# Asking for rows of the second expert table twelve rows behind the first instead of eight

## The chip, the cores and the metric

The kernel runs on one core of a Trainium2 chip. The metric is device time in microseconds for one execution. Before the change three runs gave 4503.58, 4523.78 and 4526.52 us, a median of 4523.78 us. A further, profiled execution took 4516.98 us; all rows of the trace are from it.

## The reference, cut to what matters

The program is two blocks of a transformer-like model in float32, over 512 tokens of width 1024. What the change touches is the last part of the second block, a product-key expert layer. Each token has 8 heads that choose 16 of 16,384 experts each, so 128 experts per token. An expert is one row of 1024 numbers in table `u_tab` and one in table `v_tab`:

```
t   = h.reshape(512, 1024)
idx = e1 * 128 + e2                         # (token, head, 16) expert numbers
gate = softmax(best)                        # their weights
act = gelu(einsum('phkd,pd->phk', u_tab[idx], t)) * gate
out = einsum('phk,phkd->pd', act, v_tab[idx])
x   = x + out;  then the final rmsnorm
```

So for each token 128 rows of each table are gathered from the chip's memory: 512 x 128 x 2 rows of 4 KB, 537 MB in all. That is most of what the program moves.

## The kernel before, in words

The four tiles of 128 tokens are treated one after the other. What the code calls a row `k` (0 to 511) is one gather of 128 table rows, one for each token of a tile, 512 KB: `k // 128` is the tile, `k % 128` the expert slot. For each `k` there is a U gather, a dot product, an activation, a V gather and an accumulation. Five instruction streams run over the same count of ticks, `TICKS = range(ROWS + TILE_LAG)`, 524 of them. Each stream is in order, and waits in it hold everything behind them:

- POOL (lines 1161 to 1182): at tick `k` it asks for U row `k` (line 1167) as soon as VectorE has finished the dot of row `k-8` (semaphore `u_used`), since there are `ERING = 8` U buffers. Right behind it comes V row `v = k - V_LAG` (line 1176), as soon as TensorE has used V row `v-8` (`v_used`), since there are 8 V buffers too. At ticks 39, 71, 103 and so on, every 32 rows, `expert_numbers` (lines 1141 to 1157) computes the next 32 expert numbers on the same engine; it needs what `pair_choice` left on VectorE eight ticks before.
- VectorE, called DVE (lines 2253 to 2276): at tick `k` it waits for U row `k` to land and makes the dot products (line 2262, the product is written over the row). At each eighth tick it turns the activations of the last eight rows into weights (`acts`, line 2267). Every 32 ticks come `key_choice` and `pair_choice`, the top-16 searches.
- ScalarE, called ACT (lines 1591 to 1616): at tick `k` it builds the diagonal matrix of row `k-9` (line 1601) from `acts`; at each eighth tick it does the gelu of eight dots (line 1604).
- TensorE, called PE (lines 2801 to 2836): at tick `k = v + 11`, for even `v`, it waits until V rows `v` and `v+1` have landed and their diagonals are ready, and adds both into four banks (line 2826, the trace has 16 matmuls for a pair).
- At ticks 138 and 139, and 128 and 256 later, a tile ends: ACT's `final_swap` waits until all 128 V rows of the tile are used (line 1562), PE adds the swapped halves (line 2807), ACT's `final_root` squares them (line 1576), and DVE's `final_rows` (lines 2233 to 2246) scales and writes the rows, ahead of the dot of its tick. Only then can PE take the banks for the next tile (line 2817).

Beside the gathers, tokens 256 to 511 still have to go through the whole of the second block before their own experts are known. That work, called `side` in each stream, is spread over ticks 2 to 204 (table `SIDE`): at the end of tick `k` each of PE, DVE and ACT does its share of that tick's side steps. PE's side step of a tick often feeds DVE's of the same tick, and so on. Its weights come through SP's queue in blocks of 1 MB, into two places of the ring.

The ticks are the order in which each stream writes its work; nothing makes two streams be at the same tick but the semaphores named.

Of the kernel before, what the change touches and what calls it, by code (L numbers as in the profile page):

```python
# [170 lines left out]
ERING = 8  # L171
EXPERTS = PH * PTOPK
ROWS = NL // P * EXPERTS
V_LAG, DIAG_LAG, SUM_LAG, TILE_LAG = 8, 9, 10, 12
SCORE_LEAD, KEY_LEAD, PAIR_LEAD, NUMBER_LEAD, SHARE_LEAD = 49, 41, 33, 25, 17
SIDE_COST = {"msq": 4, "msum": 34, "mscl": 4, "lruz": 4, "ab": 20, "sp1": 10, "sp2": 10, "sp3": 15, "xr": 34, "gate": 34, "lg": 14,
             "le": 10, "ls": 15, "qkv": 34, "z": 34, "gq": 4, "gs": 6, "gr": 8, "gn": 12, "ktok": 12, "vtok": 12, "pa": 40, "pb": 40, "eye": 10,
# [2680 lines left out]
```

How the kernel before makes its waits and increments, by code:

```python
        def claim(pe, t, extra=0):  # L389
            if use_of[t] > 0:
                pe.wait_ge(S(f"bank{bank_of[t]}_free"), use_of[t] + extra)
            return ps[bank_of[t]]
# [4 lines left out]
        def filled(eng, t, extra=0):  # L398
            eng.wait_ge(S(f"bank{bank_of[t]}_full"), use_of[t] + 1 + extra)
            return ps[bank_of[t]]
# [4 lines left out]
        def emptied(eng, t, extra=0):  # L406
            eng.wait_ge(S(f"bank{bank_of[t]}_free"), use_of[t] + 1 + extra)
# [33 lines left out]
        def block(pe, b, k, extra=0, n=None):  # L442
            pe.wait_ge(S(f"weights{slot_of[b]}"), 16 * (load_of[b] + 1) + 16 * extra)
            n = n or SLOT // k
            return ring_part[slot_of[b]][:, 0:k * n].rearrange("p (k n) -> p k n", k=k)
# [7 lines left out]
            def __call__(self, eng, ins):  # L454
                self.n += 1
                ins.then_inc(S(self.name), 1)
                eng.wait_ge(S(self.name), self.n + self.off)
# [115 lines left out]
        def norm_sums(pe, tag, tbs, h, kd=KD, per=1):  # L573
            t0 = ticket0[f"norm_{tag}"]
            for b, (lo, hi) in enumerate(tbs):
                bank = claim(pe, t0 + b)
                for k in range(kd):
                    pe.wait_ge(S(f"{tag}_sq"), per * k + 1 + (b if per > 1 else 0))
                    last = pe.matmul(bank[:, 0:hi - lo], ones[:, :], h[:, k, lo:hi], start=(k == 0), stop=(k == kd - 1))
                fill(last, t0 + b)
# [558 lines left out]
            def expert_numbers(u):  # L1141
                t, j = UNITS[u]
                pool.wait_ge(S("onehot_ready"), u + 1)
                for s in range(2):
```

## Time and profile before

| | us |
|---|---|
| three runs | 4503.58, 4523.78, 4526.52; median 4523.78 |
| profiled execution, its own time | 4516.98 |
| its span | 4515.1 |
| outside the span | 1.9 |
| busy: PE, DVE, POOL, ACT | 3608.2, 1988.7, 1459.2, 965.8 |
| gather instructions on POOL: U (L1167), V (L1176) | 541.2 (512 of them), 535.0 (512 of them) |

"Busy" counts the time in which an engine executes; an engine that waits for a semaphore is idle. A gather instruction on POOL only writes the descriptors; the transfer then runs on the 16 DMA engines, and "to landing" is the time from the instruction's start to the arrival of all its bytes. The first U gather starts at 2768.5 us of the span and the last V gather at 4492.9 us.

### The profile page before, as it was taken

To read this page: it belongs to the slowest core of one execution; us is meant where nothing else is said; L and a number is where in the kernel's file an instruction comes from. 1 tells how busy PE (TensorE), PEld (TensorE's weight loads), DVE (VectorE), ACT (ScalarE), POOL (GpSimd) and SP (SyncE) were. 2 spreads that over 40 slices of the span, in tenths; PEclk is the share of its full clock that TensorE was granted. 3 is DMA by queue.
4 is the path that set the end of the run, shared out by engine and by line. 5 is a ranking of instruction groups with operands and counts; after the bars stand their busy time and mean duration, and the time that the engine had idled before them with its cause. 6 is when DMAs were issued, how large, how long until landed. Compare 5 with 4: busy or idle time off the path is not lost.

```text
span 4515.1 us, 45196 instructions
## 1 busy us (share of the span) xinstructions
PE 3608.2 (80%) x16837; PEld 2076.7 (46%) x16837; DVE 1988.7 (44%) x4450; ACT 965.8 (21%) x2181; POOL 1459.2 (32%) x1670
## 2 busy tenths in 40 slices
PE   6789998999999778999997987777787765545545
PEld 3355534555555564444466876435454521111111
DVE  2565062632232682111125214676654555555553
ACT  3564022200000211100034211342222111112111
POOL 0000001253322000000000002566666677777776
PEclk8899999999999889999998999888898987767677
DMA  4232102222113124322221223987798999899998
GB/s 175 75 112 80 56 23 49 75 107 107 71 73 139 43 104 160 113 74 74 82 88 40 94 94 129 327 314 286 279 346 333 363 346 349 340 343 354 357 361 343
DMA packets 287765, 821.56 MB, mean 182 GB/s; under 512 B 24040, under 2 KB 60341, under 8 KB 284245
## 3 DMA queue, kind: packets, MB, share of 16 engines
q0 software_dynamic: 150832, 565.17, 33.3%
q1 hardware_dynamic: 136320, 253.22, 15.7%
q8 instruction: 118, 1.93, 0.2%
q14 instruction: 75, 0.61, 0.0%
q10 hardware_dynamic: 420, 0.62, 0.0%
HBM read 791.67 MB, written 27.26 MB: 181 GB/s over the span
## 4 chain that ended last, share of the span: by engine, by line
PE 61%; DVE 13%; POOL 8%; ACT 6%; issue 6%; DMA 6%; SPq 0%; ACTq 0%; DVEq 0%; POOLq 0%
PE bank L716 24%; PE bank L2593 8%; PE bank L2826 5%; POOL arena L1176 4%; POOL ring L1167 3%; PE bank L2396 3%; PE bank L2553 2%; DVE ring L2262 2%; PE bank L2448 2%; DMA ring<-in_peer_u,arena 2%; DMA arena<-in_peer_v,arena 1%; PE bank L2688 1%; PE bank L2312 1%; PE bank L581 1%; DMA ring<-in_peer_wq 1%
## 5 line engine op out<-in xcount | busy, mean ns | idle before, releaser
L2826 PE MATMUL bank<-arena 64*64 64x512 f32 x4096 | 646.4, 762 | 452.5 <-issue 205.0
L2262 DVE SCALAR_TENSOR_TENSOR ring<-ring,xT 128x1024 f32<-128x1024 f32 x512 | 634.6, 1254 | 437.7 <-DMA ring<-in_peer_u,arena 436.3
L1176 POOL DMA_INDIRECT arena<-in_peer_v,arena x512 | 535.0, 1045 | 329.5 <-PE bank L2826 199.6
L1167 POOL DMA_INDIRECT ring<-in_peer_u,arena x512 | 541.2, 1057 | 184.8 <-issue 150.9
L2826 PEld LDWEIGHTS bank<-arena 64*64 64x64 f32 x4096 | 177.3, 162 | 842.3 <-issue 840.1
L716 PE MATMUL bank<-hT,ring 128*128 128x512 f32 (+1 forms) x1536 | 554.7, 524 | 5.1 <-ACT hT L631 5.1
L716 PE MATMUL bank<-arena,ring 128*128 128x512 f32 (+1 forms) x1536 | 551.3, 521 | 0.0
L2593 PE MATMUL bank<-hT,ring 128*128 128x256 f32 x1536 | 368.4, 400 | 62.9 <-DVE hT L2002 22.4
L716 PEld LDWEIGHTS bank<-hT,ring 128*128 128x128 f32 x1536 | 293.4, 191 | 264.6 <-issue 251.5
L716 PEld LDWEIGHTS bank<-arena,ring 128*128 128x128 f32 x1536 | 292.3, 190 | 257.7 <-issue 243.9
L1148 POOL TENSOR_TENSOR hT<-hT,arena 128x256 f32<-128x256 f32 x64 | 61.1, 985 | 1069.9 <-DVE hT L2219 1069.6
L2593 PEld LDWEIGHTS bank<-hT,ring 128*128 128x128 f32 x1536 | 303.9, 201 | 142.8 <-issue 43.1
L748 DVE SCALAR_TENSOR_TENSOR xT<-bank,modT,xT 128x512 f32<-128x512 f32 x96 | 63.5, 662 | 421.2 <-PE bank L716 421.1
L728 ACT ACTIVATE arena<-bank 128x512 f32<-128x512 f32 x96 | 50.4, 526 | 905.2 <-PE bank L716 905.1
L740 DVE TENSOR_TENSOR arena<-arena 128x512 f32<-128x512 f32 x96 | 64.6, 681 | 388.4 <-ACT arena L728 387.8
L1601 ACT ACTIVATE arena<-arena,rstd 128x64 f32<-128x64 f32 x512 | 141.0, 336 | 258.9 <-DVE rstd L2267 254.9
L1078 POOL DMA_DIRECT2D arena<-shape_consts x3 | 1.6, 535 | 414.4 <-ACT arena L1278 414.4
L2396 PE MATMUL bank<-hT,ring 128*128 128x256 f32 (+1 forms) x384 | 124.3, 486 | 0.0
L2553 PE MATMUL bank<-hT,ring 128*128 128x512 f32 x256 | 111.7, 600 | 0.0
L1604 ACT ACTIVATE rstd<-rstd 128x8 f32<-128x8 f32 x64 | 13.2, 206 | 457.0 <-DVE ring L2262 456.8
L2448 PE MATMUL bank<-arena,ring 128*128 128x512 f32 (+1 forms) x256 | 88.3, 506 | 14.6 <-DVE arena L1764 14.6
L2396 PEld LDWEIGHTS bank<-hT,ring 128*128 128x128 f32 x384 | 73.0, 190 | 51.3 <-issue 46.5
(518 smaller groups left out, 4657.9 us busy)
## 6 DMA issues: line engine op xcount, KB each, us to landing
ring<-in_mlp_w SPq DMA_DIRECT2D x32, 2048.0 KB, 8.3
ring<-in_ada_w SPq DMA_DIRECT2D x24, 2048.0 KB, 11.5
s_store<-arena POOLq DMA_DIRECT2D x8, 2816.0 KB, 9.5
ring<-in_w_in SPq DMA_DIRECT2D x10, 2048.0 KB, 8.0
arena<-s_store SPq DMA_DIRECT2D x16, 1024.0 KB, 6.5
ring<-in_w_in SPq DMA_DIRECT2D x12, 1024.0 KB, 12.9
ring<-in_w_out SPq DMA_DIRECT2D x4, 2048.0 KB, 8.1
ring<-in_s_w_glu SPq DMA_DIRECT2D x4, 2048.0 KB, 17.4
```

Source lines behind the costliest of these rows:

```text
L716: last = pe.matmul(bank[:, 0:hi - lo], w[:, k, m * P:(m + 1) * P], x[:, k, lo:hi], start=(k == 0), stop=(k == 7))
L740: dve.tensor_tensor(hid[:, m, lo:hi], hid[:, m, lo:hi], hid[:, m, lo:hi], ALU.mult)\
L748: drained(dve.scalar_tensor_tensor(xT[:, m, lo:hi], bank[:, 0:hi - lo], modT[l][:, 5 * KD + m, b:b + 1], xT[:, m, lo:hi], ALU.mult, ALU.ad ...
L1167: pool.indirect_dma_start(u_row[k % ERING], None, I["peer_u_2"][0], bass.IndirectOffsetOnAxis(idxs[:, k // EXPERTS, k % EXPERTS:k % EXPERT ...
L1176: pool.indirect_dma_start(v_row[v % ERING], None, I["peer_v_2"][0], bass.IndirectOffsetOnAxis(idxs[:, v // EXPERTS, v % EXPERTS:v % EXPERT ...
L1601: act.activation(diag[:, d % ERING, :], eye2, ACT.Copy, scale=acts[:, d % ERING:d % ERING + 1]).then_inc(S("diag_ready"), 1)
L2262: dve.scalar_tensor_tensor(row, row, 1.0, h_tok[k // EXPERTS % 2], ALU.mult, ALU.mult, accum_out=dots[k // ERING % 2][:, k % ERING:k % ERI ...
L2396: last = pe.matmul(bank[:, 0:hi - lo], w[:, k, m * P:(m + 1) * P], hT[:, k, lo:hi], start=(k == 0), stop=(k == KD - 1))
L2448: last = pe.matmul(bank[:, 0:hi - lo], w[:, k, m * P:(m + 1) * P], mixT[:, k, lo:hi], start=(k == 0), stop=(k == 7))
L2553: last = pe.matmul(bank[:, :], w[half][:, k, m * P:(m + 1) * P], hT[:, k, 0:NL], start=(k == 0), stop=(k == KD - 1))
L2593: last = pe.matmul(bank[:, 0:HALF], w[:, k, c:c + P], y, start=(k == 0), stop=(k == KD - 1))
L2826: last = pe.matmul(banks[2 * r + n][QUADS[r if y == 0 else 1 - r], :], diag[QUADS[r], s, :], v_row[s][QUADS[r], 512 * n:512 * n + 512], st ...
```

## The change

It changes one constant: V row `v` is written into POOL's stream behind U row `v+12` instead of behind U row `v+8`. The first V gather comes at tick 12, the last at tick 523, which is the last tick that there is. Numbers of buffers, the other streams, their ticks and all semaphores stay. The waits in front of the V gather stay too: V row `v` still needs the buffer of V row `v-8`.

```diff
-V_LAG, DIAG_LAG, SUM_LAG, TILE_LAG = 8, 9, 10, 12
+V_LAG, DIAG_LAG, SUM_LAG, TILE_LAG = 12, 9, 10, 12
```

The only use of the constant:

```
v = k - V_LAG
if 0 <= v < ROWS:
    if v >= ERING:
        pool.wait_ge(S("v_used"), v - ERING + 1)
    ...
    pool.indirect_dma_start(v_row[v % ERING], ...)
```

## Rows read from the trace of the kernel before

**Rows 1.** The page's table of 40 slices: busy share of the DMA engines.
```profile
DMA  4232102222113124322221223987798999899998
```

**Rows 2.** Windows: stretch, length, busy us of each engine, PE clock, DMA share, GB/s.
```profile
3000.00:3200.00 200.00, 144.62 (x882) 91.28 (x881) 134.69 (x325) 61.37 (x140) 125.63 (x123) 0.82 0.74 267
...
3536.00:3600.00 64.00, 54.60 (x300) 36.74 (x299) 22.27 (x41) 11.64 (x33) 44.01 (x47) 0.97 0.93 342
3600.00:3664.00 64.00, 44.89 (x267) 22.84 (x265) 35.39 (x99) 10.56 (x33) 41.84 (x44) 0.88 0.85 315
...
4400.00:4450.00 50.00, 26.84 (x160) 7.44 (x160) 23.80 (x44) 5.96 (x25) 38.11 (x40) 0.83 1.03 409
```

**Rows 3.** POOL's waits, 2807 to 3536 us: us in total, times, longest.
```profile
POOL arena L1176 <- PE bank L2826: 159.2, 48, 18.8
POOL ring L1167 <- DVE ring L2262: 26.1, 2, 24.2
```

**Rows 4.** DVE's waits in the same stretch.
```profile
DVE xT L2150 <- PE bank L2593: 40.1, 13, 7.1
DVE ring L2262 <- DMA ring<-in_peer_u,arena: 25.1, 11, 6.4
```

**Rows 5.** POOL's waits for V buffers, 3536 to 3664 us.
```profile
POOL arena L1176 <- PE bank L2826: 30.7, 13, 7.2
```

**Rows 6.** POOL's waits for V buffers, 3664 us to the end.
```profile
POOL arena L1176 <- PE bank L2826: 16.8, 35, 2.5
```

**Rows 7.** All V gathers, source line 1176: their time to landing.
```profile
DMA to landing us min/median/max: 4.0/6.5/15.5
```

**Rows 8.** Timeline of POOL, U198 to U200: start, length, engine, line, [idle before, releaser].
```profile
3527.17 0.94 POOL L1167 DMA_INDIRECT ring<-in_peer_u,arena  x1 [0.31 <-issue]
3535.30 0.95 POOL L1176 DMA_INDIRECT arena<-in_peer_v,arena  x1 [7.19 <-PE bank L2826]
3536.55 1.98 POOL L1167 DMA_INDIRECT ring<-in_peer_u,arena  x1 [0.30 <-issue]
...
3539.80 2.77 POOL L1148 TENSOR_TENSOR hT<-hT,arena 128x256 f32<-128x256 f32 x4
...
3547.91 1.01 POOL L1167 DMA_INDIRECT ring<-in_peer_u,arena  x1 [0.51 <-POOL arena L1156]
```

**Rows 9.** Timeline of DVE, dots of rows 191 and 192.
```profile
3521.02 1.21 DVE L2262 SCALAR_TENSOR_TENSOR ring<-ring,xT 128x1024 f32<-128x1024 f32 x1
...
3530.70 1.22 DVE L2262 SCALAR_TENSOR_TENSOR ring<-ring,xT 128x1024 f32<-128x1024 f32 x1
```

**Rows 10.** Timeline of POOL, V208 and V210.
```profile
3604.36 0.94 POOL L1176 DMA_INDIRECT arena<-in_peer_v,arena  x1 [6.48 <-PE bank L2826]
...
3614.90 0.94 POOL L1176 DMA_INDIRECT arena<-in_peer_v,arena  x1 [5.60 <-PE bank L2826]
```

**Rows 11.** Timeline of PE around tick 137: V124/125 and V126/127.
```profile
3310.09 1.95 PE L2826 MATMUL bank<-arena 64*64 64x512 f32 x16
...
3319.07 1.95 PE L2826 MATMUL bank<-arena 64*64 64x512 f32 x16
```

**Rows 12.** Timeline of POOL, expert numbers of tick 135 and U136.
```profile
3299.75 4.81 POOL L1148 TENSOR_TENSOR hT<-hT,arena 128x256 f32<-128x256 f32 x4
...
3310.77 1.86 POOL L1167 DMA_INDIRECT ring<-in_peer_u,arena  x1 [0.51 <-POOL arena L1156]
```

**Rows 13.** Timeline around tick 267, the end of the second tile.
```profile
3764.29 2.41 ACT L1568 ACTIVATE arena<-bank 64x512 f32<-64x512 f32 x4
...
3767.40 1.29 POOL L1176 DMA_INDIRECT arena<-in_peer_v,arena  x1 [0.30 <-issue]
...
3777.17 1.22 DVE L2262 SCALAR_TENSOR_TENSOR ring<-ring,xT 128x1024 f32<-128x1024 f32 x1
```

**Rows 14.** Timeline of PE and POOL behind it: first matmuls of tile three, U275.
```profile
3777.06 4.68 PE L2817 MATMUL bank<-ident,xT 128*64 128x128 f32 x32 [8.26 <-DVE arena L2242]
...
3783.98 0.93 POOL L1176 DMA_INDIRECT arena<-in_peer_v,arena  x1 [2.49 <-PE bank L2826]
...
3790.39 0.94 POOL L1167 DMA_INDIRECT ring<-in_peer_u,arena  x1 [0.30 <-issue]
```

**Rows 15.** Timeline of the end: POOL's last wait, PE's last pair.
```profile
4482.65 3.69 PE L2826 MATMUL bank<-arena 64*64 64x512 f32 x16 [2.06 <-issue]
...
4491.70 0.94 POOL L1176 DMA_INDIRECT arena<-in_peer_v,arena  x1 [2.02 <-PE bank L2826]
...
4498.14 1.95 PE L2826 MATMUL bank<-arena 64*64 64x512 f32 x16 [0.81 <-issue]
```

**Rows 16.** Weight loads, whole page and 2807 to 3530 us: times, size, us to landing.
```profile
ring<-in_mlp_w SPq DMA_DIRECT2D x32, 2048.0 KB, 8.3
...
ring<-in_w_in SPq DMA_DIRECT2D x11, 1024.0 KB, 14.7
```

## The prediction

> **What bounds the kernel now.** I read the page's slices first, to see where the gathers lie. The DMA engines are busy four tenths or less of nearly every slice up to about 2800 us, and seven to nine tenths of each one after [rows 1]. The change touches nothing earlier, so the question is about the last 1707 us. Then I read POOL's waits in three stretches, since POOL's stream is what is reordered, and last the timeline at the places where it waits.
>
> From 2807 to 3536 us (ticks 8 to 199) the side work of the second half of the tokens runs beside the gathers. POOL sits 159.2 us in front of V gathers, 48 times, because PE has not used the row eight before [rows 3]. Yet DVE waits only 25.1 us, 11 times, for a U row to land [rows 4]; it waits as long on PE's side products (40.1 us for one line alone [rows 4]). Here the side work sets the pace and the gathers have room: the DMA share is 0.74 from 3000 to 3200 us [rows 2]. POOL's waits are idle time of an engine that is not the bound.
>
> From about tick 199 to the end it is the other way about. Side work ends at tick 204. A U and a V gather take POOL 2 x 0.94 us plus 2 x 0.30 us of gaps [rows 8], 2.48 us a row, and the DMA engines at their fastest, 409 GB/s [rows 2], move the 1.05 MB of a row in 2.56 us. The two limits are level, and nothing that POOL loses there is made up later. So a microsecond of POOL's wait behind tick 199 counts in full, unless the DMA engines had a backlog to live on.
>
> **What the change does to order and waits.** It removes and adds no instruction. All 1024 gathers keep their cost on POOL. V row v is asked for four U gathers later. Three limits move.
>
> (a) *The V buffer.* Before, POOL at tick k needs V row k-16, which PE uses at its tick k-5. After, it needs V row k-20, used at PE's tick k-9. POOL can't be more than eight ticks ahead of DVE anyway, because of the U buffers. So the V wait nearly always comes due before the U wait has let POOL through, and it goes as far as PE keeps with DVE. What is late next is the dot of row k-8.
>
> (b) *The landing of V.* Before, PE at tick k needs a V row that POOL asked for at tick k-2. After, at tick k+2. The rows land 6.5 us after they are asked for in the median, 15.5 at most [rows 7]. POOL runs up to eight ticks ahead, so some six ticks are left to cover that; at the 3.8 us a tick of the side stretch (727 us from U8 at 2809 to U199 at 3536, 191 rows) that is 23 us. It is enough but where POOL has just stood still for the expert numbers.
>
> (c) *The end of a tile*, where DVE's `final_rows` at tick 139 (267, 395) needs a V row that POOL asks for at tick 139 itself.
>
> **The sum, part by part.**
>
> *Ticks 8 to 199.* The 159.2 us turn into waits for dots. U rows are asked for earlier, but a gain comes only out of the 25.1 us that DVE waits for them [rows 4]: 0 to 25. Against it stands (b). At tick 137 PE used V124/125 at 3310.09 [rows 11]. V125 is now asked for at POOL's tick 137, behind the expert numbers of tick 135 and U136. Those took from 3299.75 to 3310.77 [rows 12] and can begin about 5 us earlier; so V125 goes out at 3309.4 and lands some 8 us later (the stretch is crowded), at 3317.4: PE is 7.3 us late, and the tile's end behind it, at 3319.07 before [rows 11], by up to as much. At the other five such stalls the same sum leaves V landing 1 us or more ahead of PE, or up to 3 us behind. I take a gain of 10 and a loss of 7, net -3; the ends are -25 and +20 (three stalls at 7).
>
> *Ticks 199 to 232, 3536 to 3664 us.* POOL waits 30.7 us in 13 places for V buffers [rows 5]; each has 0.3 us that any gather has before it, so 30.7 - 3.9 = 26.8 us can go. The first is V190's, 7.19 us [rows 8]: without it U199 starts at 3529.7. Its buffer is free when dot 191 ends, at 3522.2 [rows 9], so nothing takes the wait's place, and U200 behind the expert numbers comes at 3541.0 instead of 3547.91 [rows 8]; dot 192 ends at 3531.9 [rows 9]. That is 6.9 us, the lower bound. The others, above all 6.48 and 5.60 us at V208 and V210 [rows 10], fall where the DMA engines are working off a backlog of weights and rows, so they are not all worth their length. By bytes: 342 and 315 GB/s over 64 us each [rows 2] are 42.0 MB, which at 409 GB/s take 102.8 us of the 128: 25.2 us idle, of which two stalls for expert numbers keep some 6 each. That leaves 13 us, and the pauses before the rate reaches its top give back a little more as a backlog. Between 6.9 and 26.8 I take the middle, 17, near to the 13.
>
> *Ticks 232 to 511.* The waits for V buffers are 16.8 us in 35 places [rows 6]; less 35 x 0.3 they are 6.3 us, in three places: 2.49 at tick 272 [rows 14], as much at tick 400, and 2.02 at the last rows [rows 15]. They go. New ones come at the two tile ends. At tick 267 V255 goes out at 3767.40, where V259 went [rows 13], lands 6.5 us later at 3773.9, and PE is through with it at 3777. From there the chain is as before: `final_swap` began at 3764.29 and the dot of 267 at 3777.17 [rows 13], 12.9 us; so dot 267 starts at about 3790 instead of 3777. U275 needs it: it would go out at 3787.9 without V264's wait (3790.39 less 2.5 [rows 14]) and goes at 3791.3, 3.4 us late. PE's first matmuls of the next tile take 4.68 us [rows 14] and V256 is used at 3796, some 1.0 us after V264 wants its buffer. So 4.4 us at each of two ends, 8.8 us for 6.3 saved less what the end costs: there twelve V rows follow the last U row at 1.24 us each, while PE takes 1.95 or 3.69 us a pair [rows 15]; V504's buffer comes 0 to 2 us late. 1 us. Net +3.5; the ends are -6 and +12 (a full 12.9 us at one end where POOL has no slack).
>
> Sum: -3 - 17 + 3.5 = -16.5 us on the profiled execution's own 4516.98 us, 4500.5 us. That execution lies 6.8 us under the median of the runs shown; on the median it is 4507.3 us.
>
> **The rivals.**
>
> *All of it counts.* The whole 26.8 us are won, the 6.3 too, and half of DVE's 25.1. For it: behind tick 219 rows landed as soon as they could. Against it: the bytes above. -26.8 - 12.5 - 6.3 + 9.8 = -36: 4488.
>
> *The weights pay.* The blocks of weights of ticks 185 to 204 share the DMA engines with the gathers: a 2 MB load lands in 8.3 us early in the program, 1 MB loads beside the gathers in 14.7 [rows 16]. Gathers that are asked for earlier hold these loads up, PE's last side steps come later, and of the second term only its lower bound is left: -3 - 6.9 + 3.5 = -6.4, 4517. Against it: 25 us of idle DMA time are there to be used. (The Trainium skill has a rule that speaks for this rival: by its page "DMA: Bandwidth & Descriptors", section "Anatomy of one DMA", each DMA engine takes turns, packet by packet, between the queues that have work. By that rule, the trace agrees: half the bytes take longer.)
>
> *Nothing changes.* The ring is eight deep before and after, and every wait for a V buffer becomes a wait of the same length for a dot. 4524. Against it stand dots 191 and 192 [rows 9], done before their buffers are wanted.
>
> *V comes late to PE (slower).* If PE's tick in the side stretch waits for V at each of the six expert-number stalls (ticks 39 to 199) and not at one, DVE's side step waits for PE, its next dot for that, and POOL for the dot. The price is the 7.3 us of tick 137 six times, 44 us, less 17 won later: +27, 4551. It decides from the point where V lands later than the side work needs: the slack is some 5 us at such a stall, 17 elsewhere.
>
> **Chances.** Forecast 0.38 (its own range 4496 to 4520), all of it 0.29, the weights 0.10, nothing 0.05, V late 0.18. What a measurement can tell from no change is about 0.5%, 22.6 us, so faster begins at 4501: 0.29 and a tenth of a chance from the forecast's low side, 0.38 together; slower begins at 4546 but mishaps short of the full price also end there: 0.17; the rest, 0.45, is within. The range goes from a little past the second case, 4480, to 4538, half way into the fourth.
>
> **What would show it.** In the profile after: POOL's V gathers wait for PE in few places, under 20 us in excess, and its U gathers wait for L2262 many times over 100 us in all before 3536; no V wait between ticks 199 and 232; DVE's tile ends 12 us later against its dots' landing; PE waits for V landing in the side stretch at tick 137 alone. The forecast is wrong if U199 starts later than 3536 (side work hurt), or if the distance from U199 to the last V gather, 956 us now (3536.55 to 4492.9), does not shrink by some 10 us.

## The result, and the profile after

The changed kernel is slower: 4546.83 us, the median of 6 runs (4540.34 to 4556.53), against 4523.33 us for the kernel before in 6 runs (4503.58 to 4526.52). The ratio is 1.0062, with a 95% interval of 1.0040 to 1.0084. The forecast was 4507, the range ended at 4538, and the sign is the other one. The profiled execution took 4540.34 us, 23.4 us more than the profiled execution before, about as much as the medians differ (23.5), so the two traces can be compared place by place. One trace of each has its limits, though. Four traces of kernels whose gathers are in the same order up to dot 134, eight rows behind (before, and the experiments a_late12, m_onlyends and o_tail), take 503.2, 510.6, 504.2 and 500.8 us from the first dot to dot 134, and then 23.6 to 23.7 us from dot 134 to dot 140. So ten microseconds mean nothing over the long stretch and much over the short one.

First the page of the changed kernel: its span, the busy time of each engine, the slices of DMA share that answer to [rows 1], and the two groups of gathers (out<-in, count | busy us, mean ns | idle us ahead and what ended most of it).

```profile
span 4538.4 us, 45196 instructions
...
PE 3618.7 (80%) x16837; PEld 2071.9 (46%) x16837; DVE 1984.4 (44%) x4450; ACT 972.5 (21%) x2181; POOL 1484.2 (33%) x1670
...
DMA  4232102222223134222220224888888999899998
...
L1167 POOL DMA_INDIRECT ring<-in_peer_u,arena x512 | 561.3, 1096 | 321.3 <-DVE ring L2262 177.0
L1176 POOL DMA_INDIRECT arena<-in_peer_v,arena x512 | 536.3, 1047 | 174.2 <-issue 148.2
```

The DMA slices are those of before but for a digit here and there. POOL is busy for 25.0 us more than before, 20.1 of them in the U gathers (561.3 instead of 541.2). That is as long as the loss, but it isn't the loss: two kernels of the experiments, n_burstall and p_num21_after, have POOL busy for 1488.0 and 1480.0 us and are as fast as the kernel before. The time is in waits.

Then POOL's waits from 2807 to 3536 us (us in total, times, longest), which answer to [rows 3].

```profile
POOL ring L1167 <- DVE ring L2262: 166.5, 45, 25.9
POOL hT L1148 <- DVE hT L2219: 16.4, 4, 4.5
POOL arena L1176 <- PE bank L2826: 4.5, 10, 1.8
```

The 159.2 us in front of V gathers became 4.5, and the 26.1 us in front of U gathers became 166.5. (One more wait of 8.20 us, ahead of V148, is put down to nothing by the profile; V148 needs the buffer of V140, whose matmuls began at 3399.86, shortly before it went out at 3403.46.) POOL waits at least as long as before, for something else. That part went as forecast, and it is a swap, not a gain.

DVE's waits in the same stretch answer to [rows 4].

```profile
DVE xT L2150 <- PE bank L2593: 54.9, 14, 13.1
...
DVE rstd L2267 <- ACT rstd L1604: 35.6, 11, 12.7
```

DVE's wait for PE's side products rose from 40.1 to 54.9 us, and its longest single wait from 7.1 to 13.1. That one lies at tick 135. The timelines of the changed kernel there (start, length, engine, line, idle before and releaser) are the heart of the case. POOL first: U136 behind the expert numbers of tick 135, then V124, V125, U and V in turn.

```profile
3301.78 5.66 POOL L1148 TENSOR_TENSOR hT<-hT,arena 128x256 f32<-128x256 f32 x4 [3.67 <-DVE hT L2219]
3307.52 3.40 POOL L1152 TENSOR_TENSOR hT<-hT 128x512 f32<-128x512 f32 x3
...
3314.49 1.01 POOL L1167 DMA_INDIRECT ring<-in_peer_u,arena  x1 [0.51 <-POOL arena L1156]
3315.80 0.95 POOL L1176 DMA_INDIRECT arena<-in_peer_v,arena  x1 [0.30 <-issue]
...
3318.49 0.94 POOL L1176 DMA_INDIRECT arena<-in_peer_v,arena  x1 [0.30 <-issue]
```

PE in the same ticks. The first line below is V122/123, the pair ahead of V124/125; L2593 is side work; V124/125 is the one with 8.65 us of idle time before it, V126/127 the next, and L2807 is the first step of the tile's end.

```profile
3310.18 1.95 PE L2826 MATMUL bank<-arena 64*64 64x512 f32 x16
3313.89 1.89 PE L2593 MATMUL bank<-arena,ring 128*128 128x256 f32 x8
3324.43 3.46 PE L2826 MATMUL bank<-arena 64*64 64x512 f32 x16 [8.65 <-issue]
3334.92 1.95 PE L2826 MATMUL bank<-arena 64*64 64x512 f32 x16
3338.21 2.29 PE L2807 MATMUL bank<-arena,ident 64*64 64x512 f32 x8 [1.34 <-ACT arena L1568]
```

The profile names no releaser for the 8.65 us (`issue`), but the time to landing of V125's gather, taken alone, settles it. V125 was asked for at 3318.49, so it landed at 3324.3, and the pair began at 3324.43.

```profile
DMA to landing us min/median/max: 5.8/5.8/5.8
```

And DVE: its side step that waits for PE behind that pair, the wait of the tile's end, and the dot of row 139.

```profile
3331.57 0.42 DVE L2150 TENSOR_TENSOR xT<-xT,bank 128x256 f32<-128x256 f32 x1 [13.05 <-PE bank L2593]
...
3343.71 0.16 DVE L2235 TENSOR_TENSOR rstd<-rstd 128x1 f32<-128x1 f32 x1 [5.97 <-ACT arena L1576]
...
3348.87 1.23 DVE L2262 SCALAR_TENSOR_TENSOR ring<-ring,xT 128x1024 f32<-128x1024 f32 x1
```

In the trace before, V124/125 began at 3310.09 and V126/127 at 3319.07 [rows 11]. The L2150 step and the dot of row 139 stood there as follows.

```profile
3315.73 0.42 DVE L2150 TENSOR_TENSOR xT<-xT,bank 128x256 f32<-128x256 f32 x1 [2.82 <-PE bank L2593]
...
3333.01 1.23 DVE L2262 SCALAR_TENSOR_TENSOR ring<-ring,xT 128x1024 f32<-128x1024 f32 x1
```

The dot of row 139 is 15.9 us later in the changed kernel. 5.6 of that were there at dot 134 already; 10.3 arise here. The chain reads: POOL stands still for the expert numbers; V124 and V125 are now among what is queued behind them; PE stands for the pair; DVE's next side step stands for PE; POOL's next U gather stands for the dot behind it. V126/127, two ticks on, and the end of the tile inherit the delay. (The prediction gave V124/125 to PE's tick 137; since pair `v` belongs to tick `v + 11`, it is that of tick 135. Tick 137 is where POOL asks for V125. The rows and their times are the same.)

The same thing stands at the second tile's end, where [rows 13, 14] show the kernel before. PE around tick 267 (V252/253 with 10.10 us of idle time, V254/255, the tile's end, the next tile's first matmuls), then DVE:

```profile
3779.47 3.69 PE L2826 MATMUL bank<-arena 64*64 64x512 f32 x16 [10.10 <-issue]
3785.08 3.53 PE L2826 MATMUL bank<-arena 64*64 64x512 f32 x16 [1.92 <-issue]
3789.95 2.30 PE L2807 MATMUL bank<-arena,ident 64*64 64x512 f32 x8 [1.34 <-ACT arena L1568]
...
3800.50 4.68 PE L2817 MATMUL bank<-ident,xT 128*64 128x128 f32 x32 [8.26 <-DVE arena L2242]
```
```profile
3795.45 0.16 DVE L2235 TENSOR_TENSOR rstd<-rstd 128x1 f32<-128x1 f32 x1 [13.14 <-ACT arena L1576]
```

The serial chain itself is as long as before (8.26 us ahead of L2817 in both traces). It starts later, and DVE waits 13.14 us in it.

Last the windows (stretch, length, busy us of each engine, PE clock, DMA share, GB/s). The first three answer to [rows 2]. The other two have the 128 us from the start of U199, first in the kernel before, then in the changed one; 34 U and 34 V gathers start in each.

```profile
3000.00:3200.00 200.00, 141.74 (x896) 89.68 (x890) 139.06 (x334) 64.75 (x148) 136.63 (x128) 0.85 0.79 282
3536.00:3600.00 64.00, 50.05 (x262) 30.19 (x258) 38.59 (x80) 10.77 (x28) 52.48 (x48) 0.92 0.88 333
3600.00:3664.00 64.00, 52.06 (x308) 32.22 (x311) 38.19 (x107) 13.48 (x42) 43.31 (x40) 0.96 1.03 394
...
3536.55:3664.55 128.00, 98.95 (x562) 59.09 (x561) 57.11 (x140) 22.21 (x66) 86.15 (x90) 0.93 0.89 329
...
3546.85:3674.85 128.00, 101.53 (x560) 61.05 (x560) 68.50 (x160) 22.95 (x68) 96.80 (x90) 0.92 0.89 337
```

The window behind 3600 us carries 394 GB/s where it carried 315, as if the second term of the forecast were there. But U199 starts 10.3 us later in the changed kernel, so windows at equal times show different work. From U199 on the DMA engines move 337 GB/s instead of 329, and U232 starts 125.7 us behind U199 instead of 125.8. POOL waits 16.5 us less for V buffers in that stretch (7.0 instead of 23.5), and nothing is won. It waits 4.0 us for a dot instead, it is busy for 10.7 us more (96.80 instead of 86.15), and a U row lands 9.7 us behind its gather in the median instead of 7.2.

The prediction named two signs of being wrong, and both are there: U199 starts at 3546.85, later than 3536, and from U199 to the last V gather it takes 968.4 us where it took 956.4.

To place the 23.4 us I took the distance between the starts of the same two dots in both traces:

```
dots          before    after    difference
134 to 140      23.6     33.9     +10.3   (end of tile one)
168 to 232     219.8    212.9      -6.9
264 to 296      96.8    101.3      +4.5   (behind the end of tile two)
last dot to last V gather
                 6.5     11.4      +4.9
```

What these four rows leave (+10.6 us) is spread: +5.6 up to dot 134, +1.2 between 140 and 168, +1.4 from 232 to 264, +3.2 from 296 to 392, -1.7 from there to dot 511, and some 1 us behind the last V gather. The last two rows of the small table belong together in part: four V rows that stand behind twelve U rows instead of eight are four times 1.24 us of POOL's stream, 5.0 us, put off from the rows' side to the end. So of the 6.9 us "won" between dots 168 and 232, 5.0 could be such a debt, and the tail of +4.9 is where it is paid. The +5.6 up to dot 134 is within what separates traces of one order of gathers.

### The profile page after: what moved, and what is told of

Its sections match the earlier page's. It is cut to its first block, busy times and chain, and to the rows that moved or that the text cites. A ratio compares the mean times of both kernels' runs of the same rounds, so it can differ in the third digit from the quotient of the medians.

```text
span 4538.4 us, 45196 instructions
## 1 busy us (share of the span) xinstructions
PE 3618.7 (80%) x16837; PEld 2071.9 (46%) x16837; DVE 1984.4 (44%) x4450; ACT 972.5 (21%) x2181; POOL 1484.2 (33%) x1670
## 4 chain that ended last, share of the span: by engine, by line
PE 61%; DVE 11%; POOL 9%; issue 7%; DMA 6%; ACT 6%; SPq 0%; DVEq 0%; ACTq 0%; POOLq 0%
PE bank L716 24%; PE bank L2593 8%; PE bank L2826 6%; POOL ring L1167 4%; POOL arena L1176 4%; DMA arena<-in_peer_v,arena 3%; PE bank L2396 3%; PE bank L2553 2%; PE bank L2448 2%; DVE ring L2262 1%; PE bank L2688 1%; PE bank L2312 1%; DMA ring<-in_peer_wq 1%; PE bank L581 1%; PE bank L2388 1%
## 5 line engine op out<-in xcount | busy, mean ns | idle before, releaser
L2826 PE MATMUL bank<-arena 64*64 64x512 f32 x4096 | 658.8, 771 | 479.4 <-issue 397.2
L1167 POOL DMA_INDIRECT ring<-in_peer_u,arena x512 | 561.3, 1096 | 321.3 <-DVE ring L2262 177.0
L2593 PE MATMUL bank<-hT,ring 128*128 128x256 f32 x1536 | 368.5, 399 | 61.5 <-DMA ring<-in_peer_wq 20.3
L2593 PEld LDWEIGHTS bank<-hT,ring 128*128 128x128 f32 x1536 | 303.0, 201 | 142.3 <-issue 41.4
L2593 PE MATMUL bank<-arena,ring 128*128 128x256 f32 x384 | 89.9, 388 | 4.2 <-DMA ring<-in_xattn_wo 3.5
## 6 DMA issues: line engine op xcount, KB each, us to landing
ring<-in_w_in SPq DMA_DIRECT2D x12, 1024.0 KB, 10.3
```

Of the source, the lines that this page charges most:

```text
L1167: pool.indirect_dma_start(u_row[k % ERING], None, I["peer_u_2"][0], bass.IndirectOffsetOnAxis(idxs[:, k // EXPERTS, k % EXPERTS:k % EXPERT ...
L2593: last = pe.matmul(bank[:, 0:HALF], w[:, k, c:c + P], y, start=(k == 0), stop=(k == KD - 1))
L2826: last = pe.matmul(banks[2 * r + n][QUADS[r if y == 0 else 1 - r], :], diag[QUADS[r], s, :], v_row[s][QUADS[r], 512 * n:512 * n + 512], st ...
```

## The experiments

Each was timed beside the kernel before. In two of the sessions (e to h, i to l) that kernel took 4599 and 4613 us instead of 4523 to 4525, so only the ratios are compared. A ratio of 0.001 is 4.5 us, and the intervals are some 0.0015 to 0.002 to either side: two results less than about 10 us apart aren't told from each other.

Most kernels use one tool: POOL's lag as a function of its tick. This is its diff, with the function of the first experiment.

```diff
+def v_asked():
+    asked, v = {}, 0
+    for k in range(ROWS + TILE_LAG):
+        upto = min(k - v_lag(k), ROWS - 1)
+        while v <= upto:
+            asked.setdefault(k, []).append(v)
+            v += 1
+    return asked
+
+def v_lag(k):
+    return 8 if k < 208 else 12
...
-                v = k - V_LAG
-                if 0 <= v < ROWS:
+                for v in V_ASKED.get(k, ()):
```

Where the lag falls from 12 to 8 for a tick, five V rows are asked for in that tick, behind its U row and ahead of its expert numbers; in the four ticks behind it, when the lag is 12 again, none is. I call that asking early. Where the lag falls from 12 to 8 for good, the same five gathers stand at one tick with no pause behind them; I call that catching up.

**Which half of the run costs?** The change behind tick 208 alone, and the change up to there alone.

```diff
+    return 8 if k < 208 else 12
```

> V rows are asked for eight rows behind U up to tick 207 and twelve behind from tick 212 on; four ticks without a V gather lie between. Theory 1 (V rows land too late for PE and ACT while the side work runs): the side stretch is as in the kernel before, so the time is the kernel before's plus at most what the tile ends and the last rows cost, +3 to +8 us of the +23.5. Rival 2 (the loss is the longer way of a V row at the tile ends, at the last rows and in every gelu chain behind tick 208): most of the loss stays, +15 or more. Rival 3 (my second term was right and only hidden by the side stretch): a little faster than before, -5 to -15.

```diff
+    return 12 if k < 208 else 8
```

> The other half: twelve behind up to tick 207, then five V gathers at tick 208 and eight behind from there. Theory 1: nearly the whole loss stays, +15 to +25 us against the kernel before. Rival 2: under +8. If the two halves add up to the whole, nothing but their own stretch matters.

Measured: 1.0014 (1.0000 to 1.0029) for the late half, some 6 us; 1.0042 (1.0024 to 1.0061) for the side stretch, some 19 us. Together they make 25 of the 28 us that the whole ratio is. Most of the loss is where the side work runs.

**The whole change at other sizes.** Lags of ten and of six throughout.

```diff
-V_LAG, DIAG_LAG, SUM_LAG, TILE_LAG = 12, 9, 10, 12
+V_LAG, DIAG_LAG, SUM_LAG, TILE_LAG = 10, 9, 10, 12
```

> Ten rows behind, throughout. Theory 1: V rows lose two ticks (some 7.6 us in the side stretch) of their lead instead of four, and the slack at an expert-number stall is about 5 us, so the loss is small: 0 to +8 us against the kernel before. A rival in which each tick of lag costs the same says +12. A rival in which the loss comes from U rows being asked for earlier (they crowd out the weight loads) says nearly the whole +20, since at ten most of the waits for V buffers are gone already.

```diff
-V_LAG, DIAG_LAG, SUM_LAG, TILE_LAG = 12, 9, 10, 12
+V_LAG, DIAG_LAG, SUM_LAG, TILE_LAG = 6, 9, 10, 12
```

> Six rows behind, throughout. If a V row's lead over its use is what costs and eight has enough of it, nothing is won and POOL's wait for V buffers grows by two ticks: +2 to +12 us against the kernel before. If time goes straight with the lag (12: +28, 10: +3, 8: 0), this is 0 to -5. It tells whether eight lies on the flat part of the curve.

Measured: 1.0006 (0.9991 to 1.0022) for ten, 1.0055 (1.0036 to 1.0073) for six. The curve is flat between eight and ten and costs 25 us (six) and 28 us (twelve) two rows beyond on either side. With ten, dots 134 to 140 take 23.7 us, as with eight: V124 and V125 go out ahead of the expert numbers of tick 135 (135 - 10 = 125), and with twelve they go out behind. No experiment isolates what sets six back. Its trace shows POOL waiting 265.2 us for V buffers and DVE 544.0 us for U rows to land, against 217.8 and 436.5 us in f_acts_before, a kernel with eight rows on the same chip.

**Is it the place behind the expert numbers?** The change, but with the V rows asked for early at the six stalls of the side stretch.

```diff
+    return 8 if 39 <= k < 208 and k % 32 == 7 else 12
```

> Twelve rows behind, but at ticks 39, 71, 103, 135, 167 and 199, ahead of the expert numbers, POOL asks for the next four V rows at once (back to eight behind), and for none in the four ticks after. Only the V rows that the stall would hold up come early. Theory 1 in its narrow form (the loss is PE waiting for V rows held up by the expert numbers, 4.3 + 8.7 + 2.5 us in the trace): the time falls by 12 to 20 us against the changed kernel, to within +8 of the kernel before. In its wide form (V is late everywhere in the side stretch, through ACT's diagonals and the gelu too): by less than 8. Rival, crowding of the weight loads: no change.

Measured: 1.0027 (1.0007 to 1.0047) against 1.0062. More than half of the loss went, and dots 134 to 140 took 23.7 us again. Some 12 us stayed.

**Is it ScalarE's gelu that DVE waits for?** DVE's wait for L1604 grew by 14 us in the first trace (21.4 to 35.6 us in the side stretch). That rival says that ScalarE comes late to its gelu, held up in its stream by a diagonal that waits for the use of a late V row. The two kernels put `acts` one tick later, on the changed kernel and on the kernel before.

```diff
-                if k % ERING == 0 and 0 < k <= ROWS:
+                if k % ERING == 1 and ERING <= k < ROWS + ERING:
```

> The changed kernel, but DVE turns eight activations into weights one tick later (ticks 9, 17, ...), behind the next dot, so that it does not stand still for ACT's gelu, which is behind a diagonal that waits for a V row's use. In the changed kernel's trace DVE waits 123 us for the gelu in all, 45 us before the change. Theory 2 (V late, hence ACT late, hence DVE late costs time beside the stalls at the expert numbers): the changed kernel gets 5 to 15 us faster. Theory 1 alone (only PE's waits for V at the stalls count): the change is under 4 us.

> The same move in the kernel before. If the wait for the gelu costs as much there (45 us of waits), this gains too, 2 to 6 us, and the gain of the run above is not the change's. If the coupling is the change's, 0 plus or minus 4.

Measured: 1.0064 (1.0047 to 1.0082) on the change, 1.0015 (1.0000 to 1.0031) on the kernel before. Between the two lie 0.0049, some 22 us: the loss is nearly unmoved. The edit took away only part of the wait, though: in the side stretch 19.6 us of it are left of 35.6, and over all the gathers there are 125 us as before it (123). What speaks against the rival more strongly is further down: n_burstall and p_num21_after wait 124.7 and 139.0 us for this gelu and lose nothing. That wait was a place where DVE's time showed, not where it was made.

**Early in the side stretch, eight behind it.** By the first experiments this should cost nearly nothing.

```diff
+    return 8 if k >= 208 or 39 <= k and k % 32 == 7 else 12
```

> Twelve behind with the four early V gathers ahead of each expert-number stall up to tick 207, and eight behind after that: the burst kernel without its late half. The burst kernel is 12 us over the kernel before, the late half alone cost 6. If the two add up, this is +3 to +8 against the kernel before; if the burst takes away all of the side stretch's loss, 0 to +3; if U rows asked for earlier are worth anything, as my prediction had it, it is faster than the kernel before, -3 to -12.

Measured: 1.0028 (1.0015 to 1.0041), 13 us. This was missed, and no run explains it. One thing that its trace shows: from dot 204 to dot 232 it takes 106.4 us, b_side12 with the same fall from twelve to eight at tick 208 takes 106.9, and five traces with eight rows there take 96.3 to 100.1 (before, f_acts_before, j_only135, m_onlyends, o_tail). The four V gathers that are caught up at tick 208 may be what costs there; then some of b_side12's 19 us is that too, and not the change's. The kernels j_only135, l_mid12 and m_onlyends below catch up as well, at ticks 140, 231, 268 and 396, so the same doubt hangs on their prices. Against it stands n_burstall, which asks for five V rows at once 14 times and loses nothing, but pauses behind each.

**One place at a time.** The changed kernel with tick 135 repaired; the kernel before with only ticks 129 to 139 made late; the changed kernel with the three tile ends repaired.

```diff
+    return 8 if k == 135 else 12
```

> The changed kernel with one place altered: at tick 135 V124 to V127 are asked for at once, ahead of the expert numbers, and none in ticks 136 to 139. In all traces with twelve rows of lag in the side stretch the dots of rows 134 and 140 stand 33.9 to 36.3 us apart, and 23.6 to 23.8 with eight, ten or the burst. If that is the step it costs 10 us of the change's 23.5 to 28: this run is 8 to 13 us faster than the changed kernel, ratio to the kernel before 1.003 to 1.0045. If what is lost there is won back behind it (the side work has room), it stays at 1.006.

```diff
+    return 12 if 129 <= k < 140 else 8
```

> The kernel before with the same place altered the other way: twelve behind from tick 129 to 139 alone, so that V124 to V127 are asked for behind the stall, eight behind elsewhere. By the theory of the one place: +8 to +13 us against the kernel before (ratio 1.002 to 1.003). By 'V late everywhere': under +4.

```diff
+    return 8 if k in (135, 263, 391) else 12
```

> The changed kernel with the four V gathers early at ticks 135, 263 and 391, ahead of the expert numbers just before each of the three tile ends. The dots of rows 264 and 272 stand 31.2 to 35.0 us apart where the lag is twelve behind tick 208, 25.4 to 26.3 where it is eight. Theory: 3 to 6 us more than the run above. Rival (DVE makes up the lateness from the eight U buffers): 0 to 2 more.

Measured: 1.0052 (1.0032 to 1.0072), 1.0036 (1.0019 to 1.0053) and 1.0029 (1.0011 to 1.0048). Eleven ticks of late V rows in an otherwise unchanged kernel cost 14 to 16 us by themselves. PE in that kernel (lines numbered 17 higher): V124/125, the tile's end, then the next tile's first matmuls.

```profile
3358.18 3.69 PE L2843 MATMUL bank<-arena 64*64 64x512 f32 x16 [9.31 <-issue]
...
3375.56 2.85 PE L2824 MATMUL bank<-arena,ident 64*64 64x512 f32 x8 [2.26 <-ACT arena L1585]
...
3386.66 4.48 PE L2834 MATMUL bank<-ident,xT 128*64 128x128 f32 x32 [8.25 <-DVE arena L2259]
```

The 9.31 us idle is the 8.65 of the changed kernel, with the same chain behind; dots 134 to 140 take 38.7 us. Repairing that one place in the changed kernel gives back its 10 us there (23.7 us again), but the timed whole only moved from 1.0062 to 1.0052, short of what was expected, and its dots 392 to 400 took 41.0 us against 31.5. With all three tile ends repaired 13 us are left. What holds them isn't shown: repairing all stalls (n_burstall) takes them away, but so does p_num21_after, in which V rows still stand behind every stall that isn't at a tile's end.

**The terms of the forecast by themselves.** The second term (ticks 199 to 232) alone, the two later tile ends alone, and the tail alone.

```diff
+    return 12 if 186 <= k < 231 else 8
```

> The second term of my prediction by itself: eight behind, but twelve from tick 186 to 230, where POOL waited 26.8 us for V buffers, and back to eight at tick 231 ahead of the expert numbers. As predicted, 7 to 27 us faster than the kernel before, 17 likeliest. By the changed kernel's trace, in which the dots of rows 168 and 232 stand 212.9 us apart instead of 219.8, and by 5 us of V gathers put off in it: 2 us faster, which is no difference that can be told.

```diff
+    return 12 if 257 <= k < 268 or 385 <= k < 396 else 8
```

> The kernel before, with twelve rows of lag at the two later tile ends alone (ticks 257 to 267 and 385 to 395), so that the last four V rows of tiles two and three are asked for behind the expert numbers. The prediction has 4.4 us for each such end, less 2.2 of a wait that goes: +4 for both. The stretch of dots 264 to 272 alone says +6 to +10 each if nothing is made up behind it: +12 to +20. If DVE makes it up out of its eight U buffers: 0 to +5.

```diff
+    return 12 if k >= 490 else 8
```

> Eight behind, but twelve from tick 490 on: only the last rows are put off, and twelve V gathers instead of eight stand behind the last U gather. By the prediction +1 us. In the changed kernel's trace the last V gather starts 11.4 us behind the last dot's start instead of 6.5, but that dot has four V gathers less, 5.0 us, ahead of it: -0.1, no difference. A rival: PE is slow there and V buffers come late, +3 to +5.

Measured: 1.0005 (0.9989 to 1.0021), 1.0025 (1.0007 to 1.0042) and 0.9994 (0.9980 to 1.0009). The term of -17 us is worth nothing that can be measured. (l_mid12 also catches up, at tick 231. In its trace U232 starts 131.7 us behind U199, and 5.0 of those are the four V gathers caught up; that leaves 126.7, where f_acts_before and j_only135, with eight rows there and on the same chip, take 127.4 and 126.3.) The two tile ends cost 11 us, with an interval from 3 to 19, and the tail nothing.

**All stalls at once.** Early at every stall from tick 39 on, 14 of them, twelve rows behind everywhere else.

```diff
+    return 8 if k >= 39 and k % 32 == 7 else 12
```

> The changed kernel with the four V gathers early at every one of the expert-number stalls from tick 39 on, 14 places. With all places mended, what is left of the +28 us is what a lag of twelve costs away from the stalls. If V rows held up by stalls are the whole cause: -3 to +5 us against the kernel before. If there is a cost in the side stretch that no stall explains, as the two burst kernels suggest (both +12): +8 to +14.

Measured: 0.9999 (0.9987 to 1.0012). The whole loss is gone, though seven of eight V gathers still go out twelve rows behind. PE in this kernel at ticks 133 to 137: V124/125 is the second of three pairs.

```profile
3309.80 1.95 PE L2843 MATMUL bank<-arena 64*64 64x512 f32 x16
...
3315.32 1.95 PE L2843 MATMUL bank<-arena 64*64 64x512 f32 x16
...
3324.31 1.95 PE L2843 MATMUL bank<-arena 64*64 64x512 f32 x16
```

No pair has idle time before it. And POOL's waits from 2807 us to the end:

```profile
POOL ring L1185 <- DVE ring L2279: 152.1, 38, 25.7
POOL arena L1193 <- PE bank L2843: 58.4, 52, 11.1
```

POOL now has 210 us of waits (226 in the kernel before), and the kernel is as fast as the one before. Asking for V later neither costs nor brings anything once no V row stands behind a stall.

**Move the stall instead of the V rows.** The expert numbers come four ticks later, at ticks 43, 75, ..., 139, so that V127, V255 and V383 are ahead of them with a lag of twelve too. The same edit on the kernel before is the control.

```diff
-SCORE_LEAD, KEY_LEAD, PAIR_LEAD, NUMBER_LEAD, SHARE_LEAD = 49, 41, 33, 25, 17
+SCORE_LEAD, KEY_LEAD, PAIR_LEAD, NUMBER_LEAD, SHARE_LEAD = 49, 41, 33, 21, 17
```

> The changed kernel with the stall itself moved: POOL computes the expert numbers four ticks later (ticks 43, 75, ..., 139, ...), behind V127, V255 and V383 instead of ahead of V124, V252 and V380. Theory (V rows held up by the stall just ahead of a tile end): most of the loss goes, ratio to the kernel before 0.998 to 1.002. Rival (any V row held up by any stall costs, wherever it stands): the stalls hold up other V rows, and it stays at 1.004 or more.

> The control: the same move in the kernel before, where V124 to V127 are asked for at ticks 132 to 135, ahead of the stall in either place. Theory: no difference, 0.999 to 1.001. If it gains, the move is worth something by itself and is the version that beats both.

Measured: 0.9990 (0.9976 to 1.0004) on the change, 0.9996 (0.9982 to 1.0010) on the kernel before. PE of the changed kernel with the moved stall, at the end of tile one and at the head of tile two:

```profile
3309.59 2.29 PE L2807 MATMUL bank<-arena,ident 64*64 64x512 f32 x8 [1.34 <-ACT arena L1568]
...
3320.14 4.68 PE L2817 MATMUL bank<-ident,xT 128*64 128x128 f32 x32 [8.26 <-DVE arena L2242]
```

The end of the tile begins at 3309.59, 28.6 us ahead of the changed kernel's 3338.21. Of these, 18.6 us are there at dot 134 already; the other 10 are this place's, where dots 134 to 140 take no more than 23.8 us. With twelve rows and the stall moved, nothing of the 28 us is left, and this is the lowest of all ratios, though its interval reaches over 1. None of the 17 kernels is shown to beat the kernel before.

Two things in this pair matter for the reading. The moved stall still holds up V rows, only others: PE waits 5.5 us for V64/65 at tick 75 and 4.4 us for V96/97 at tick 107, and 10 to 12 us at each of six later stalls, with no loss. So a late V row that isn't ahead of a tile's end need not cost. And in the control, dots 134 to 140 take 31.2 us at no cost in time, so that distance alone is no proof of a loss either. The edit also gives the expert numbers four more ticks behind `pair_choice`: POOL waited for it 16.4 us in four places in the changed kernel, and doesn't here. That wait by itself isn't the loss, since c_lag10 has 10.7 us of it, in the same four places, and 1.0006.

## Why the prediction was wrong

*The swap of waits in (a)* was right: V waits gone at POOL, U waits over 100 us in their place.

*Ticks 8 to 199, -3 us.* This is one of the two steps that failed. It was put at -3 us and measured +19 alone (b_side12); together with the other step, put at -17 and measured +2, that is about the 39.5 us by which the forecast missed. Its mechanism (b) was right: V125 behind the expert numbers of tick 135, and PE idle for it. That the idle time is 8.65 us where 7.3 was said is partly luck. V125 was asked for at 3318.49, 9.1 us later than the 3309.4 of the forecast; but it landed in 5.8 us instead of 8, and PE was 5.7 us later itself. The price was mis-sized. I wrote that the tile's end behind it would be late "by up to as much", and took 7. The dots' distance at that place grew by 10.3 us in the changed kernel and by 15 in the kernel with that place alone, and it cost 14 to 16 us timed. Two things make it more than its idle time. The pair behind, V126/127, is late as well, and behind that stands the end of the tile, in which PE, ACT and DVE work in turn. And the stall itself moved: its expert numbers began at 3301.78 where they had begun at 3299.75 [rows 12], where I had let them start 5 us earlier. They waited 3.67 us for DVE's `pair_choice`, a wait that an earlier POOL can't shorten. The gain of 10 us that was set against it never came, either: with every stall repaired the kernel is as fast as the one before (0.9999) and not 10 us faster. The side work set the pace, as my first part said, and I still let U rows that come earlier count for 10.

*The other five stalls of that stretch* were put at "up to 3 us behind" and then at nothing. With the three tile ends repaired 13 us stayed, with all 14 stalls repaired none. The places aren't told apart finer than that. The trace shows one of them, V60/61 at tick 71 behind the expert numbers of that tick, where PE waits 4.2 us more than before; it waits 2.5 us more at tick 191 too, at no stall. So "PE waits for V landing in the side stretch at tick 137 alone" was wrong, but p_num21_after waits as long at such places (17.9 us in the side stretch, counting waits of over 1.5 us, against 16.1) and loses nothing.

*Ticks 199 to 232, -17 us.* This is the other step that failed. I counted POOL's waits and idle DMA time as if removing the one would fill the other. POOL's waits for V did go, and the DMA engines moved hardly more for it (337 GB/s instead of 329 from U199 on), and U199 to U232 took 125.7 us instead of 125.8. In place of the waits stood a wait for a dot, longer work of POOL, and U rows that landed later. Alone this part measured 1.0005, +2 us, with an interval from -5 to +10 us, and so lies outside even its lower bound of 6.9. In the trace dots 168 to 232 gain 6.9 us, 5.0 of which are V gathers put off, and the tail gives back 4.9. Why gathers and expert numbers take longer there wasn't isolated.

*Ticks 232 to 511, +3.5 us.* The form was right (V255 late, the chain behind it unchanged). The size was perhaps too small: net 4.4 us each less what was saved, about 4 us for both, against 11 measured alone. But the interval of the 11 reaches down to 3, and the whole late half, a_late12, measured 6 us with 0 to 13, so 3.5 isn't refuted. The 1 us for the tail was about right: nothing measured, since the 4.9 us later last V gather are the put-off gathers.

*The rivals.* "V comes late to PE" had the right sign, and 4551 stands 4 us from the result, but by a sum that the runs don't bear out: 44 us less 17. What was measured is some 15 to 19 us in the side stretch, 11 at two tile ends, and no 17 us to set against them. "All of it counts" failed with the second term. "The weights pay" had nothing for it: with ten rows, or with all stalls repaired, the loads share the DMA engines with U gathers asked for earlier than before, and the time is that of before. (The rule that it cites from the Trainium skill, page "DMA: Bandwidth & Descriptors", stands in the section "Queues, rings and completion order" and not in "Anatomy of one DMA". That half the bytes took longer agrees with it, but no run here tests the turns.) "Nothing changes" was right about the waits, which turned into waits for dots, and missed the late rows.

*What stays open:* the 13 us of the kernel that is early in the side stretch and at eight behind it; the 13 us that stay with the three tile ends repaired, though moving the stall away from those ends leaves none; why the change at six rows costs 25 us; how much of the prices of j_only135 (14 to 16 us) and m_onlyends (11) is their catching up; and how the loss in the side stretch is shared among its six stalls, since one by itself cost 14 to 16 us and its repair in company perhaps 5.

## What to carry to other kernels

How far behind another stream a request is put is not a matter of its mean lead. Write out the order at each fixed stall of the engine that issues it, and see which requests change from ahead of the stall to behind it; two rows more cost nothing here, four cost 28 us, because of what then stood behind the stalls, above all just ahead of a tile's end. Price a late request by what is serial behind its consumer (here the end of a tile), not by its own delay; and before a wait that is removed is booked as a gain, ask whether its engine sets the pace there. Compare two traces from the same instruction on, and not at the same time: 315 against 394 GB/s was a shift of 10 us, and 329 against 337 was what there was.

## What was not expected of the hardware

VectorE and GpSimd slow each other when both compute. The same dot takes 1.22 us alone and 1.74 us beside GpSimd's expert numbers, and GpSimd's four products of the expert numbers take 2.77 us where VectorE is quiet [rows 8], but 4.81 us [rows 12], 5.66 us (above) and, at 3056.68 us in the trace before, 5.90 us beside dots. It isn't always shared: at 3427.61 us in the trace before, the four products took 2.76 us and the one dot beside them 4.34. So the length of the very stall that this case turns on depends on what VectorE does beside it. The mechanism was not tested.

The kernel before took 4523 to 4525 us in some sessions and 4599 or 4613 in two others, 1.6 to 2% more. Those two ran on one and the same chip, the others for which the record names the chip on two other ones. The traces show no difference up to the first dot (2807.3 us in the kernel before, 2807.8 in f_acts_before) and all of it behind. Whether it is the chip, and what is slower there, isn't known. The change's effect of 0.6% could not have been read across sessions.
